# At the turn from one row half to the other, two operand sums and three tile sums move from VectorE to GpSimd

## What is computed

```python
xn = rmsnorm(h, norm1_g)
proj = xn @ w_in                      # q, k, v, g, z, conv columns
o_gla = gla_chunked(q, k, v, log_a)   # gated linear attention, 4 heads
o_conv = silu(channel_group_norm(causal_depthwise_conv(u)))
h = h + concat(o_gla, o_conv) @ w_out
hn = rmsnorm(h, norm2_g)
ff = square(relu(hn @ w_mlp_in))      # 2048 x 4096
h = h + ff @ w_mlp_out
return rmsnorm(h, final_norm_g)
```

## Time and profile before

| | us |
|---|---|
| median of 3 runs | 2025.66 |
| lowest, highest | 2024.34, 2025.87 |
| the profiled execution's own time | 2024.25 |
| its span, first to last instruction | 2022.2 |
| PE busy in the span | 2000.1 (99%) |
| DVE busy | 1473.9 (73%) |
| ACT busy | 956.6 (47%) |
| POOL busy | 445.9 (22%) |

### The profile page before, as it was taken

How to read it: one execution, slowest core, us unless ns; L and a number is a source line. 1 busy time by engine, 2 the same in 40 slices (tenths; PEclk the granted TensorE clock), 3 DMA queues, 4 the chain that set the end, 5 groups by cost and what they waited for, 6 DMA issues and landing times.

```text
span 2022.2 us, 27147 instructions
## 1 busy us (share of the span) xinstructions
PE 2000.1 (99%) x9898; PEld 1635.4 (81%) x9898; DVE 1473.9 (73%) x2178; ACT 956.6 (47%) x1361; POOL 445.9 (22%) x593
## 2 busy tenths in 40 slices
PE   8999999999999999999999999999999999999998
PEld 7787778787877778888888888888888888888887
DVE  3899978887878978877789777777664646545475
ACT  4456664355244563565557645554332333323253
POOL 5553475235126441000000000000020201202031
PEclk9999999999999999999999999999999999999999
DMA  6884458555555555444445433335967557565674
GB/s 227 285 289 152 139 202 295 167 168 186 198 200 191 179 208 191 162 146 144 148 163 206 153 122 127 126 121 197 376 231 266 188 203 265 181 220 185 206 239 177
DMA packets 175268, 395.76 MB, mean 196 GB/s; under 512 B 15424, under 2 KB 64672, under 8 KB 174624
## 3 DMA queue, kind: packets, MB, share of 16 engines
q1 hardware_dynamic: 154688, 317.47, 46.3%
q10 hardware_dynamic: 20448, 76.56, 10.8%
HBM read 301.70 MB, written 92.27 MB: 195 GB/s over the span
## 4 chain that ended last, share of the span: by engine, by line
PE 90%; DVE 6%; issue 2%; ACT 2%; POOL 0%; DMA 0%; DVEq 0%; ACTq 0%; POOLq 0%
PE acc L83 24%; PE acc L85 24%; PE acc L84 24%; PE acc L2565 3%; PE acc L2566 3%; PE acc L2567 3%; DVE acc L1724 2%; PE acc L2625 1%; PE acc L2520 1%; PE acc L2519 1%; PE acc L2521 1%; PE acc L2284 1%; ACT ring_hi L1355 1%; PE acc L2658 1%; DVE ring_sum L1869 1%
## 5 line engine op out<-in xcount | busy, mean ns | idle before, releaser
L1986 DVE TENSOR_TENSOR down_lo<-down_raw,down_hi 128x1536 fp32r<-128x1536 f32 x112 | 200.5, 1790 | 231.1 <-ACT down_hi L1441 231.1
L84 PE MATMUL acc<-down_lo,down_hi 128*128 128x512 f32 x896 | 348.5, 389 | 0.0
L83 PE MATMUL acc<-down_hi 128*128 128x512 f32 x896 | 348.5, 389 | 0.0
L85 PE MATMUL acc<-down_hi,down_lo 128*128 128x512 f32 x896 | 348.5, 389 | 0.0
L1441 ACT ACTIVATE down_hi<-down_raw 128x1536 fp32r<-128x1536 f32 x112 | 166.7, 1488 | 360.8 <-PE acc L85 192.9
L1724 DVE SCALAR_TENSOR_TENSOR acc<-u_sb,cw_col,acc 128x512 f32<-128x512 f32 x464 | 312.9, 747 | 0.3
L1355 ACT ACTIVATE ring_hi<-ring_sum 128x512 fp32r<-128x512 f32 x155 | 97.8, 631 | 250.3 <-DVE ring_sum L1869 247.9
L83 PE MATMUL acc<-xT_hi,wt 128*128 128x512 f32 x512 | 203.6, 398 | 0.7 <-ACT q_sb L1534 0.7
L1100 POOL TENSOR_TENSOR rows_a<-rows_a,second 128x512 f32<-128x512 f32 x20 | 25.3, 1296 | 803.6 <-ACT second L1449 655.5
L84 PE MATMUL acc<-xT_lo,wt 128*128 128x512 f32 x512 | 199.5, 390 | 0.0
L85 PE MATMUL acc<-xT_hi,wt 128*128 128x512 f32 x512 | 199.5, 390 | 0.0
(11 more groups left out here) (304 smaller groups left out, 4113.2 us busy)
## 6 DMA issues: line engine op xcount, KB each, us to landing
wt<-w_kept SPq DMA_DIRECT2D x168, 512.0 KB, 3.3
down_raw<-f_kept ACTq DMA_DIRECT2D x109, 512.0 KB, 4.3
raw_w<-in_w_mlp_in SPq DMA_DIRECT2D x32, 1024.0 KB, 5.9
f_kept<-f_tile SPq DMA_DIRECT2D x128, 256.0 KB, 2.0
down_raw<-in_w_mlp_out SPq DMA_DIRECT2D x64, 512.0 KB, 3.6
w_kept<-wt SPq DMA_DIRECT2D x48, 512.0 KB, 5.3
down_raw<-in_w_mlp_out SPq DMA_DIRECT2D x64, 256.0 KB, 3.2
down_more<-f_kept ACTq DMA_DIRECT2D x29, 512.0 KB, 5.3
```

The costliest lines, as they stand in the source:

```text
L83: nc.tensor.matmul(out, w_hi, x_hi, start=first, stop=False, skip_group_check=onto)
L84: nc.tensor.matmul(out, w_hi, x_lo, start=False, stop=False, skip_group_check=onto)
L85: return nc.tensor.matmul(out, w_lo, x_hi, start=False, stop=last, skip_group_check=onto)
L1986: nc.vector.tensor_tensor(down_lo[slot][:, :], down_raw[d % DOWN_RAW][:, 512:], down_hi[slot][:, :].bitcast(F32), ALU.subtract).then_inc(d ...
```

## The change

- `add_again` leaves VectorE and goes to GpSimd, ahead of the tile sums: four `tensor_tensor` of 128x1024 that wait for `pre_sum`'s halves and for product m of group 14.
- The three tile sums of group 14 go from VectorE's slots 0 to 2 of group 15 to GpSimd, behind those four.
- `low_again` signals after each half; the product waits for the first half at its start and for the second before its third quarter.
- `MUL_AGAIN` has product 4 ahead of product 5: the high part of 4 moves from slot (0, 0) to (-1, 6), that of 5 with its load from (-1, 6) to (0, 0).
- The load of product 7 moves from slot (0, 1) to the head of slot (0, 0).

```diff
@@ gpsimd
+            def add_again(m):
+                pool.wait_ge(mul_sum_ok, len(MUL_FIRST) + MUL_SUM_AGAIN.index(m))
+                pool.wait_ge(pre_ok, len(PRE_SUM_AT))
+                pool.wait_ge(prod_pe, used(m))
+                src, op = (h12, ALU.add) if m == 6 else (h21, ALU.subtract)
+                for part in range(2):
+                    c = slice(2 * part, 2 * part + 2)
+                    ins = nc.gpsimd.tensor_tensor(mul_sum[m][:, c, :], src[:, c, :], sum1_again[part][:, :, :], op)
+                ins.then_inc(mul_sum_ok, 1)
             def up_pass():
                 for s in range(NS):
                     up_group(s)
+                for m in MUL_SUM_AGAIN:
+                    add_again(m)
+                late_sums(group(TURN) - 1)
@@ scalar
+            def low_load(m):
+                act.wait_ge(prod_pe, used(m))
+                i = PRE_LOW.index(m)
+                act.wait_ge(pre_st, 16 * (2 * i + 2))
+                act.dma_start(mul_lo[m].bitcast(F32), mul_kept[i]).then_inc(mul_ld[m], 16)
             def mul_again(m):
                 act.wait_ge(prod_pe, used(m))
                 if m in PRE_LOW:
-                    i = PRE_LOW.index(m)
-                    act.wait_ge(pre_st, 16 * (2 * i + 2))
-                    act.dma_start(mul_lo[m].bitcast(F32), mul_kept[i]).then_inc(mul_ld[m], 16)
+                    if m != LATE_LOAD:
+                        low_load(m)
...
                         j = NQ * s + k + UP_LEAD
+                        if (s - TURN, k) == (0, 0):
+                            low_load(LATE_LOAD)
                         if j < NQ * NS:
                             a_split(j)
@@ vector
-                    ins = nc.vector.tensor_tensor(mul_lo[m][:, c, :], src, mul_hi[m][:, c, :].bitcast(F32), ALU.subtract)
-                ins.then_inc(mul_lo_v, 1)
+                    nc.vector.tensor_tensor(mul_lo[m][:, c, :], src, mul_hi[m][:, c, :].bitcast(F32),
+                                            ALU.subtract).then_inc(mul_lo_v, 1)
-            def add_again(m):
...
-                        if k in F_SUM_AT:
+                        if k in F_SUM_AT and s != TURN:
                             f_sum(group(s) - 1, F_SUMS[F_SUM_AT.index(k)])
@@ tensor
-                    pe.wait_ge(mul_lo_v, MUL_LO_AGAIN[m])
+                    pe.wait_ge(mul_lo_v, MUL_LO_AGAIN[m] - 1)
...
+                    if s == TURN and m in MUL_LO_AGAIN and k == 2:
+                        pe.wait_ge(mul_lo_v, MUL_LO_AGAIN[m])
@@ tables
-MUL_AGAIN = (2, 3, 1, 6, 5, 4, 7)
+MUL_AGAIN = (2, 3, 1, 6, 4, 5, 7)
-ADD_AGAIN_AT = {6: (-1, 3), 4: (-1, 6)}
-MUL_LO_AGAIN = {1: 6, 6: 7, 4: 8}
+MUL_LO_AGAIN = {1: 7, 6: 9, 4: 11}
+LATE_LOAD = 7
```

More of the change, by code:

```diff
@@ L1435, in down_split @@
                 if d < 2:
-                    act.wait_ge(mul_lo_v, len(MUL_LO_FIRST) + len(MUL_LO_AGAIN))
+                    act.wait_ge(mul_lo_v, len(MUL_LO_FIRST) + 2 * len(MUL_LO_AGAIN))
                 elif d < RING:
@@ L1838, in turn @@
                     pre_sum(PRE_SUM_AT.index((s, k)))
-                for m in MUL_SUM_AGAIN:
-                    if (s - TURN, k) == ADD_AGAIN_AT[m]:
-                        add_again(m)
                 for m in LOW_AGAIN_AT:
```

## The result

| | before | after |
|---|---|---|
| median of the runs | 2024.34 us (9 runs, 2024.19 to 2025.87) | 2030.32 us (9 runs, 2029.14 to 2032.02) |
| profiled execution | 2024.25 us, span 2022.2 | 2030.0 us, span 2028.3 |
| mean granted clock of TensorE | 0.999 | 0.997 |

The ratio of the times is 1.0027, with a 95% interval of 1.0017 to 1.0037: **6.0 us slower**. The interval lies above 1; its lower end, 0.17%, is just under the 0.2% that the forecast counted as a difference. Forecast were 2031.7 us and +6.0 us. The runs of before that stand beside it have a median 1.3 us lower than the one the forecast started from, so the difference came out as forecast, and the time 1.4 us lower.

The account below looks back on a forecast made before the run. TensorE, working 99% of the span, was taken to bound the kernel. A 6.7 us gap plus 1.4 of small gaps made 8.1, against the old 2.08: +6.0 on 2025.66 gave 2031.7 us, range 2027.5 to 2035.5.

Parts of the forecast that it names:

- What bounds, and what there was to gain: TensorE bounds the kernel; its three gaps from group 15 to group 16, 2.08 us, are the most to gain.
- The exclusion: At the turn, GpSimd's adds and VectorE's instructions with two SBUF inputs alternate, each holding the other for its whole length.
- B: At the turn GpSimd's work hides and the kernel is not slower: 2023.6 us; chance 0.12.
- C: At the turn a 128x1024 GpSimd add holds VectorE for only about 1.27 us: 2025.6 to 2028.7 us; chance 0.1.
- The sum of the waits: Five VectorE waits from 1091.9 us on, 9.65 us, less 2.35 of adds saved, start combine(14, 5) 7.3 us later.
- The forecast's own case: TensorE stands 6.6 us ahead of slot 1 of group 15, clock at full: +6.0 us, 2031.7 us; chance 0.48.
- rival A: The clock falls to 1.2 GHz in the gap at slot 1 of group 15: +7.3 to +10.0 us; chance 0.3.
- the small gaps: Three later TensorE gaps, behind slot 1 of group 15 up to slot 0 of group 16: 1.4 us with restarts.
- the old gap: TensorE's forecast wait ahead of slot 1 of group 15: 6.6 us, 6.7 with the restart.
- The load of product 5: Issued at about 1114.3, wanted by slot 5 at 1120.3, landing at 1119.5 to 1121.8: 0 to 1.5 us more.
- The stores behind the tile sums: Behind tile sums 1 and 6, ending near 1115.5, stores need 3 us; the next writer comes past 1123.
- The wait by halves: One semaphore wait in mid-product at the turn, claimed to cost nothing that could be seen.

Follow-up runs that it names:

- the filled gap: The changed kernel plus 22 matmuls that nobody reads, between slots 0 and 1 of group 15: 2028.83 us.
- GpSimd reads: The changed kernel with its sums back on VectorE, plus eight useless GpSimd adds of two SBUF inputs at the turn: 2032.13 us.
- VectorE only: The changed kernel with all sums back on VectorE, product 5 ahead of 4 again, group 14's tile sums one slot later: 2023.98 us.
- GpSimd writes: The changed kernel with its sums back on VectorE, plus eight GpSimd memsets to an unread scratch tile at the turn: 2025.23 us.

## Why the prediction was right

**What bounds, and what there was to gain.** Right. All of the difference lies between 1099.7 and 1126.8, and the lowest median of any kernel is 0.4 us under before, not told apart from it, of the 2.08 that were named as the most.

**The exclusion.** Right, and the step that decided. GpSimd's adds start at 1091.88 (expected near 1091.9) and lead to 1102.78, close to 11 us of them; `ring_sum` takes 2.88 (expected about 3). For a GpSimd instruction of 128x1024 there had been no row, only 128x512 in rows 7 and 8; the hold has its whole length. Rivals B and C, a hidden or a half hold, needed `ring_sum` at 0.68 or near 2: both fell.

**The sum of the waits.** Five waits of 9.65 us were forecast, and they were 8.5. The term that was mis-sized is the GpSimd add. It was taken as 2.45 us, between rows of 2.38 and 2.53; the four take 10.90 us with three VectorE instructions of 0.6 between them, so (10.90 - 1.8) / 4 = **2.27 us**, below both ends. That is 0.7 of the 1.15 us; the rest is spread over single waits. `combine(14, 5)` came at 1106.60 instead of 1107.6, and slot 1 stood 5.7 us instead of 6.6.

**The clock.** The forecast's own case had it at full, and rival A, with a chance of 0.3, had it fall. A's mechanism came true. It was said to cost 2.7 to 5.4 us, one to two whole products at the lower level, for which there was no row; it cost 2.3, eleven matmuls and so less than one product, and it did cover the small gaps, as A said: 1.4 had been forecast, the filled gap showed 0.9 and the changed kernel none. The Trainium skill ("TensorE: Matmul & The Clock Gate", Why this matters for your kernels) says that an idle gap that is long enough puts the clock back; the trace agrees, 0.50 behind a gap of 5.6 us.

**So the number was met by terms that cancel.** Forecast: 6.7 of gap + 1.4 of small gaps + 0 of clock = 8.1. Measured: 5.7 + 0 + 2.3 = 8.1, with the rounding. The mechanism of the wait was right; that its sum came out to 0.1 us was luck. Had only the add been sized right, the forecast's own case would have given 5.7 + 0.9 - 2.1 = +4.5, which is what the filled gap measured; had A alone been right, as it was priced and with the old gap, +7.3 or more. That A deserved more than 0.3 is the lesson: a gap of three times anything seen, with a known second level of the clock, was the likelier way.

**The load of product 5.** Forecast to be issued at about 1114.3, with up to 1.5 us to pay. It cost nothing. The two loads' instructions stand on ScalarE's queue at 1110.11 and 1110.73, long before the split (1112.30) and `part_v` (1112.82) that are ahead of the second in the code: the issue did not wait for the activations in front of it to run. By line 1345, issue to landing of all four loads (before); the load of 7 took 5.3, that of 5 took 8.7:

```profile
DMA to landing us min/median/max: 5.3/7.0/8.7
```

8.7 from 1110.73 ends at 1119.4, ahead of slot 5 at 1121.39. So the load went out 3.6 us sooner than forecast and took longer than the forecast's 5.2 to 7.5 us, and the one made up for the other. The stores behind the tile sums, taken at 3 us, took 6.5 to 8.1; no wait of VectorE for them shows.

**The wait by halves** was priced at nothing that could be seen. No run has it alone. The kernel without GpSimd agrees: with halves, order and loads alone it takes 2024.87 against 2024.34, no difference by its interval.

## What to carry to other kernels

GpSimd is no free second VectorE: an elementwise operation with two SBUF inputs that takes VectorE 1.2 us held VectorE's next one for 2.2 us when it was moved, so by these rows such a move could pay only where VectorE idles or reads PSUM meanwhile, which no run here tried. Before such a move, list what VectorE does in those microseconds and how many of its instructions have two SBUF inputs; if it must be moved, small pieces hold it for less (1.78 instead of 2.88 us) and here cost 2027.0 us instead of 2030.3. And where TensorE is busy 99% of the time, price a new gap twice, by its length and by the matmuls behind it at the lower clock.

## What was not expected of the hardware

- **The clock fell behind gaps of 2 us, and their length alone does not decide.** At the turn, gaps of 5.6, 4.8, 4.5, 2.3 and 1.9 us were followed by a granted clock of 0.50; the one of 1.9 had a gap of 0.4 us some 7 us ahead of it. Gaps of 1.6 us (GpSimd reads) and 1.3 us (VectorE only) were not, nor the 1.8 us wait of the earlier trace rows. But in the trace of "GpSimd writes" the clock fell at 214 us, far from the turn (0.58 and 0.57 in the stretches from 214 to 218), behind gaps of 1.17 and 0.54 us. The changed kernel has gaps of 1.18 and 0.54 at the same two places and kept 1.00. So the same gaps can go either way; what decides was not tried.
- **A fall of the clock elsewhere can cover a small difference.** The one at 214 us put what follows it 1.5 us later (the product behind it starts at 221.33 instead of 219.87), as much as separates some of the kernels here. The nine runs of the changed kernel go from 2029.14 us at a mean clock of 0.999 to 2032.02 at 0.996. The kernel before, whose trace has no fall at the turn, spreads too, from 2023.98 to 2026.12 us in the runs beside the experiments, its four slowest beside the last four kernels at 0.997. How much of the spread of the changed kernel comes from the turn is not shown.
- **GpSimd's adds of 128x1024 are faster than its other operation of that size**, 2.27 us, as worked out above, against 2.38 and 3.12.
- **The releaser in the profile was not the one in the code** at the decisive gap: `ring_lo` was named where the wait was for the ReLU that ended 0.15 us earlier. Both follow the same late VectorE, so the reading stood.
